# Two transformer blocks on one core: the opening steps of the weight pipeline, piece by piece and in another order

## What is computed

```
h = rms_norm(x, attn_norm_w[l])
proj = h @ w_in[l]
q, k, v, u, g = jnp.split(proj, splits, axis=-1)
...
lam = (exp(sum(lam_q1 * lam_k1)) - exp(sum(lam_q2 * lam_k2)) + lam_init)
a = diff_attention(q[0], q[1], k[0], k[1], v, lam, rel_bias)
...
u_a, u_b = jnp.split(u, 2, axis=-1)
c = causal_depthwise_conv(u_a * sigmoid(u_b), conv_w[l], conv_b[l])
```

## Time and profile before

| | us |
|---|---|
| median of 3 timed runs | 762.36 |
| lowest and highest of them | 761.44, 762.84 |
| the profiled execution | 763.56 |
| its span in the trace | 761.8 |
| PE busy in it | 736.0 (97%) |
| DVE, ACT, POOL busy | 483.4, 397.1, 174.5 |

### The profile page before, as it was taken

How to read it: one execution, slowest core, us unless ns; L and a number is a source line. 1 busy time by engine, 2 the same in 40 slices (tenths; PEclk the granted TensorE clock), 3 DMA queues, 4 the chain that set the end, 5 groups by cost and what they waited for, 6 DMA issues and landing times.

```text
span 761.8 us, 9087 instructions
## 1 busy us (share of the span) xinstructions
PE 736.0 (97%) x3430; PEld 597.5 (78%) x3430; DVE 483.4 (63%) x664; ACT 397.1 (52%) x521; POOL 174.5 (23%) x124
## 2 busy tenths in 40 slices
PE   5979999999999999999999999999999999999998
PEld 4868777777877888888888888877778888888886
DVE  4697785999967656555556354677746655653531
ACT  5544667575487455444445354569845455443330
POOL 1368899897700003000000000150001000000000
PEclk9989999999999999999999999999999999999999
DMA  9865444453536555655664656644334556455530
GB/s 292 227 189 165 154 158 160 150 192 128 186 131 247 194 166 169 197 187 170 199 198 142 218 164 195 208 141 149 111 111 160 171 166 196 167 190 192 195 138 28
DMA packets 81899, 131.44 MB, mean 173 GB/s; under 512 B 3888, under 2 KB 34632, under 8 KB 81856
## 3 DMA queue, kind: packets, MB, share of 16 engines
q1 hardware_dynamic: 81200, 129.25, 51.7%
q0 software_dynamic: 576, 1.35, 0.9%
q10 hardware_dynamic: 80, 0.26, 0.1%
HBM read 129.60 MB, written 1.25 MB: 172 GB/s over the span
## 4 chain that ended last, share of the span: by engine, by line
PE 73%; DVE 11%; ACT 9%; DMA 3%; issue 2%; POOL 1%; SPq 0%; ACTq 0%; DVEq 0%; POOLq 0%
PE acc L1535 22%; PE acc L1537 22%; PE acc L1536 22%; DVE aux L909 5%; PE aux L1216 4%; DMA raw<-w_in_dram 3%; ACT w_hi L556 3%; DVE w_lo L865 2%; PE aux L1259 1%; DVE gates L1046 1%; ACT conv L807 1%; POOL w_lo L541 0%; ACT L702 0%; ACT k_t L610 0%; DVE conv L1124 0%
## 5 line engine op out<-in xcount | busy, mean ns | idle before, releaser
L865 DVE TENSOR_TENSOR w_lo<-raw,w_hi 128x2048 fp32r<-128x2048 f32 x98 | 223.0, 2276 | 130.9 <-ACT w_hi L556 130.9
L556 ACT ACTIVATE w_hi<-raw 128x2048 fp32r<-128x2048 f32 (+1 forms) x119 | 225.7, 1899 | 144.6 <-PE acc L1537 133.4
L1535 PE MATMUL acc<-w_hi,h_hi 128*128 128x512 f32 x640 | 257.7, 403 | 7.7 <-DVE tok L920 4.4
L1537 PE MATMUL acc<-w_hi,h_lo 128*128 128x512 f32 x640 | 251.0, 392 | 0.0
L1536 PE MATMUL acc<-w_lo,h_hi 128*128 128x512 f32 x640 | 250.2, 391 | 0.0
L1535 PEld LDWEIGHTS acc<-w_hi,h_hi 128*128 128x128 f32 x640 | 121.1, 189 | 33.1 <-DVE tok L920 4.9
L1537 PEld LDWEIGHTS acc<-w_hi,h_lo 128*128 128x128 f32 x640 | 120.7, 189 | 26.4
L1536 PEld LDWEIGHTS acc<-w_lo,h_hi 128*128 128x128 f32 x640 | 121.0, 189 | 23.3
L541 POOL TENSOR_TENSOR w_lo<-raw,w_hi 128x2048 fp32r<-128x2048 f32 x21 | 96.7, 4604 | 4.7 <-ACT w_hi L556 4.7
L909 DVE SCALAR_TENSOR_TENSOR aux<-glu_t,vec_t,aux 128x256 f32<-128x256 f32 x232 | 94.3, 484 | 0.0
L446 POOL TENSOR_TENSOR rstd<-ms,nhalf 128x2 f32<-128x2 f32 x4 | 8.7, 2183 | 351.3 <-DVE ms L892 351.3
(11 more groups left out here) (218 smaller groups left out, 643.8 us busy)
## 6 DMA issues: line engine op xcount, KB each, us to landing
raw<-w_in_dram SPq DMA_DIRECT2D x30, 1024.0 KB, 5.2
raw<-w_down_dram SPq DMA_DIRECT2D x26, 1024.0 KB, 5.0
raw<-w_gate_up_dram SPq DMA_DIRECT2D x44, 512.0 KB, 4.7
raw<-w_up_dram SPq DMA_DIRECT2D x16, 1024.0 KB, 5.4
raw<-w_in_dram SPq DMA_DIRECT2D x16, 512.0 KB, 6.2
raw<-w_out_dram SPq DMA_DIRECT2D x8, 1024.0 KB, 5.1
raw<-w_proj_attn_dram SPq DMA_DIRECT2D x4, 1024.0 KB, 5.1
raw<-w_proj_conv_dram SPq DMA_DIRECT2D x4, 1024.0 KB, 5.1
```

The source lines that it names most:

```text
L556: nc.scalar.activation(w_hi[:, u % SPLIT, 0:nk, :], raw[:, u % RAW, 0:nk, :], ACT.Copy)\
L865: nc.vector.tensor_tensor(w_lo[:, u % SPLIT, 0:nk, :], raw[:, u % RAW, 0:nk, :], f(w_hi[:, u % SPLIT, 0:nk, :]), ALU.subtract).then_inc(w_ ...
L1535: nc.tensor.matmul(o, x_h, w_hi[:, slot, j, :], start=begin_, stop=False)
L1537: mm = nc.tensor.matmul(o, x_l, w_hi[:, slot, j, :], start=False, stop=end_)
```

## The change

It touches only steps 0 to 6. x is loaded by halves of its columns instead of by token tile. Units 0 and 1 are loaded by k-tile, eight DMAs of 256 KB, each with a semaphore of its own; the second half of x stands between the second and the third of them. Unit 1 is rounded and subtracted by k-tile as unit 0 is, and PE waits for it by k-tile. PE turns only pairs 0 and 1 of x ahead of unit 0, and pairs 2 and 3 in the middle of it, with the matmul of the bias table behind them (now in PSUM bank 3). ACT copies the table before unit 1, and squares x by token tile around the rounding of unit 2. DVE subtracts unit 2 ahead of the mean square. POOL writes the table to DRAM ahead of its power for `rstd`, and reads it back in steps 2 to 5 instead of 1 to 4.

```diff
@@ SP
-            for t in range(NT):
-                sp.dma_start(x_in[:, t, :], x_rows[:, t, :]).then_inc(x_loaded[t], 16)
+            def piece(u, kt):
+                c, k0 = units[u][:2]
+                _, _, w, col, pair, _, _ = chunks[c]
+                n = w.shape[-1]
+                src = bass.AP(tensor=w.tensor, offset=w.offset + (k0 + kt) * P * n + col,
+                              ap=[[n, P], [pair, 2], [1, CW // 2]])
+                sp.dma_start(raw[:, u, kt, :].rearrange("p (a b) -> p a b", a=2), src).then_inc(piece_in[UK * u + kt], 16)
+
+            for hf in range(2):
+                cols = slice(CW * hf, CW * (hf + 1))
+                sp.dma_start(x_in[:, :, cols], x_rows[:, :, cols]).then_inc(x_loaded[hf], 16)
+                piece(0, 2 * hf)
+                piece(0, 2 * hf + 1)
+            for kt in range(UK):
+                piece(1, kt)
@@ POOL
-            power(rstd[:, 0, :], ms[:, 0, :], mean_sq, 1, rstd_ready)
-            qk_epsilon(0)
-
             pool.wait_ge(rel_kept, 1)
             pool.dma_start(rel_dram.ap().rearrange("(h q r) -> h q r", h=H, q=SHIFTS), again(rel_row[:, :], SHIFTS))\
                 .then_inc(rel_stored, 16)
 
+            power(rstd[:, 0, :], ms[:, 0, :], mean_sq, 1, rstd_ready)
+            qk_epsilon(0)
+
-                for r in range(2 * s - 2, 2 * s) if 1 <= s <= step // 2 else ():
+                for r in range(2 * s - 4, 2 * s - 2) if 2 <= s <= step // 2 + 1 else ():
@@ ACT
-            def first_high(kt):
-                act.wait_ge(raw_in[0], raw_value[0])
-                nc.scalar.activation(w_hi[:, 0, kt, :], raw[:, 0, kt, :], ACT.Copy)\
+            def first_high(u, kt):
+                act.wait_ge(piece_in[UK * u + kt], 16)
+                nc.scalar.activation(w_hi[:, u, kt, :], raw[:, u, kt, :], ACT.Copy)\
                     .then_inc(first_hi if kt < UK - 1 else w_hi_ready, 1)
...
             stage_high(0, 3)
-            split_high(1)
-
-            for t in range(NT):
-                act.wait_ge(x_loaded[t], 16)
-                for hf in range(2):
...
+            act.wait_ge(rel_made, 1)
+            nc.scalar.activation(rel_row[:, :], aux[0:H, 3, 0:RELS], ACT.Copy).then_inc(rel_kept, 1)
+            for kt in range(UK):
+                first_high(1, kt)
+            row_squares(0)
+            split_high(2)
+            row_squares(1)
@@ DVE
-            split_low(1)
+            for kt in range(UK):
+                first_low(1, kt)
+            split_low(2)
             mean_square(0)
@@ PE
             def halfway(s):
+                if s == 0:
+                    stage(0, (2, 3))
+                    pe.wait_ge(consts_loaded, 32)
+                    pe.wait_ge(zeros_ready, 5)
+                    claim([3], rel_kept, 1)
+                    nc.tensor.matmul(aux[0:H, 3, 0:RELS], rel_aug[:, :], onehot[:, :], start=True, stop=True)\
+                        .then_inc(rel_made, 1)
...
-            stage(0, range(4))
+            stage(0, (0, 1))
...
-                        pe.wait_ge(*((first_lo, j + 1) if j < UK - 1 else (w_lo_dve, 1)))
+                    if s < PIECED:
+                        pe.wait_ge(*((first_lo, (UK - 1) * s + j + 1) if j < UK - 1 else (w_lo_dve, s + 1)))
```

More of the change, by code:

```diff
@@ L105, in build @@
     LEAD = 2
+    PIECED = 2
     raw_value = []
     for u, (c, *_) in enumerate(units):
[L110 removed]
+        raw_value.append((raw_value[u - RAW] if u >= RAW else 0)
+                         + (0 if u < PIECED else 16 if chunks[c][4] is None else 32))
     B = begin["x2", 0]
@@ L265, in build @@
         raw_in = [sem(f"raw_in{i}") for i in range(RAW)]
-        x_loaded = [sem(f"x_loaded{t}") for t in range(NT)]
+        x_loaded = [sem(f"x_loaded{hf}") for hf in range(2)]
+        piece_in = [sem(f"piece_in{k}") for k in range(PIECED * UK)]
         vecs_loaded, consts_loaded = sem("vecs_loaded"), sem("consts_loaded")
@@ L557, in split_high, with row_squares @@
                     .then_inc(w_hi_ready, 1)
-            def first_high(kt):
-                act.wait_ge(raw_in[0], raw_value[0])
-                nc.scalar.activation(w_hi[:, 0, kt, :], raw[:, 0, kt, :], ACT.Copy)\
+            def first_high(u, kt):
+                act.wait_ge(piece_in[UK * u + kt], 16)
+                nc.scalar.activation(w_hi[:, u, kt, :], raw[:, u, kt, :], ACT.Copy)\
                     .then_inc(first_hi if kt < UK - 1 else w_hi_ready, 1)
+            def row_squares(t):
+                for hf in range(2):
+                    act.wait_ge(x_loaded[hf], 16)
+                    if t or hf:
+                        act.wait_ge(squares, 2 * t + hf)
+                    nc.scalar.activation(junk[:, :], x_in[:, t, CW * hf:CW * (hf + 1)], ACT.Square,
+                                         accum_out=ss[:, 0, hf, t:t + 1]).then_inc(squares, 1)
             def stage_high(st, g):
@@ L583, in _ @@
                     stage_high(0, kt // 2)
[L584 removed]
+                first_high(0, kt)
             stage_high(0, 2)
             stage_high(0, 3)
[L587 to L595 removed]
+            act.wait_ge(rel_made, 1)
[5 more added lines that the diff above has]
+            row_squares(1)
             nc.scalar.activation(gains[:, 0:1], vcol(R_SUB, 0), ACT.Copy, scale=1.0 - LAM_INIT).then_inc(gains_ready, 1)
@@ L645, in _ @@
             for s in range(NU + 1):
-                if s == 1:
-                    act.wait_ge(rel_made, 1)
-                    nc.scalar.activation(rel_row[:, :], aux[0:H, 2, 0:RELS], ACT.Copy).then_inc(rel_kept, 1)
                 if s == 2:
@@ L686, in _ @@
                             .then_inc(probs_kept, 1)
-                if (s < EARLY or s >= B) and s != LN + 3 and s not in NORMS and s + LEAD < NU:
+                if (0 < s < EARLY or s >= B) and s != LN + 3 and s not in NORMS and s + LEAD < NU:
                     split_high(s + LEAD)
@@ L1080, in _ @@
                                 .then_inc(branch_sum, 1)
-                if s + LEAD < NU and s not in NORMS and s != LN + 3 and not on_pool(s + LEAD):
+                if 0 < s and s + LEAD < NU and s not in NORMS and s != LN + 3 and not on_pool(s + LEAD):
                     split_low(s + LEAD)
@@ L1232, in stage @@
                 src = x_res if st else x_in
+                if st == 0:
+                    pe.wait_ge(x_loaded[pairs[0] // 2], 16)
                 for g in pairs:
@@ L1428, in after @@
             def after(s):
-                if s == 0:
-                    pe.wait_ge(consts_loaded, 32)
-                    pe.wait_ge(zeros_ready, 5)
-                    claim([2], rel_kept, 1)
-                    nc.tensor.matmul(aux[0:H, 2, 0:RELS], rel_aug[:, :], onehot[:, :], start=True, stop=True)\
-                        .then_inc(rel_made, 1)
                 if s == 1:
@@ L1500, in _ @@
             mm.then_inc(vec_turned, 1)
-            for t in range(NT):
-                pe.wait_ge(x_loaded[t], 16)
-            stage(0, range(4))
+            stage(0, (0, 1))
             held[CONV_BANK] = (conv_done, CONV_OPS)
```

17 lines of the change are left out of this document (7 added, 10 removed).

## The result

The changed kernel takes **763.80 us** (median of 6 runs, 763.41 to 764.52) where the kernel before, in the runs beside it, takes 761.41 (6 runs, 761.06 to 762.84): a ratio of 1.0025 with a 95% interval of 1.0013 to 1.0037. Forecast were 757.6, with a range of 755.9 to 760.6. So it is 0.25% slower where it should have been 0.6% faster, and outside the range. The profiled execution has a span of 762.8, that of the kernel before had 761.8.

A forecast was written before the change was run, and what follows sets the result against it. PE, busy 97%, bounds the kernel, so gains come from its waits or clock. Unit 6 starts 3.1 us earlier, full clock saves about 3.0, POOL's limit leaves 4.8: median 762.36 becomes 757.6, range 755.9 to 760.6.

The forecast's parts named there:

- The start: Opening: with unit 0 loaded by k-tile, the first product starts near 10.8, 1.4 us earlier.
- The clock under the first products: Rival, opening: clock low until about 14 cuts the gain to 3.1 us (759.3), up to 6 us to 1.7; chance 0.13.
- The new wait for `lam`: Ahead of unit 2: PE waits about 1 us for DVE, leaving 0.2 of the 1.5 us gained.
- With the write out of the way: Middle: earlier table write helps unit 6's load take 7 us, not 13.35; DVE's idle 3.27 us goes.
- Unit 6's load by spread reads: Middle: one pair of reads beside this load instead of three; ACT rounds unit 6 at 36.1 without waiting for it.
- The gap ahead of unit 6 and its clock: Unit 6 starts at 48.9, 3.1 us earlier, behind 1.7 us of gap; clock stays full; rival that it falls: 0.07.
- The price of the low clock: Behind the gap ahead of unit 6: half clock costs products and transposes 2.5 + 0.4, about 3.0 us.
- POOL as the next bound: Ahead of unit 8: PE waits 1.25 us for `tok` of k(0), two reads adding 1.05; gain 4.8, not 6.0.
- The rival on the slower side: Middle: unit 6's load takes 13.35 us whatever the reads do, giving 763.7; late load chance 0.12, one third of it slower.

The follow-up runs named there:

- e9: e2 with the bias table's copy, write, eight reads and matmul back at their places of the kernel before; 756.04 us, 0.9931 of the kernel before.
- e2: e1 with all four pairs of x turned by PE ahead of unit 0; 759.92 us, 0.9973 of the kernel before.
- e1: Changed kernel with x loaded by token tile again, both loads ahead of unit 0's pieces; 762.14 us, 0.9997 of the kernel before.
- e7: Changed kernel with the table's copy, write, reads and matmul back at their places of before; 760.41 us, 0.9976 of the kernel before.
- e4: Kernel before with only the bias table's part of the change added; 762.88 us, 1.0012 of the kernel before.
- e3: Changed kernel with eight useless transposes on PE while it waits for the first piece; 761.73 us, 0.9998 of the kernel before.
- e11: e2 without the eight reads of the bias table, its write kept, zeros as bias; 759.46 us, 0.9964 of the kernel before.
- e5: e2 without the bias table's write and its eight reads, zeros as bias; 756.23 us, 0.9918 of the kernel before.
- e8: The kernel before, word for word, run again for a second trace; 761.66 us, ratio 0.9989.
- e10: e9 with the table's reads two by two in steps 2 to 5; 756.93 us, 0.9945 of the kernel before.

## Why the prediction was wrong, step by step

**Put together**, the runs lead from the kernel before to the changed one in four steps: the pieces and the new order on ACT and DVE (e9) -0.69%; the table part (e2 against e9) +0.42%; turning two pairs only ahead of unit 0 (e1 against e2) +0.24%; x by column halves (changed kernel against e1) +0.28%. That they add up to the measured +0.25% is so by construction and confirms nothing, and what a part is worth depends on the rest: the table part costs 0.49% in the changed kernel (e7) and 0.12% or nothing in the kernel before (e4). The first step was not split further, so no run says what of it the pieces gain and what the order. The prediction had the first part for the smaller gain, the second for the larger one, the third only as a rival, and the fourth not at all.

- **The start** (first product at 10.8). Right for the pieces, as e1 shows with 10.68. The step that failed is one that isn't there: the prediction looked at bytes ahead of the first piece of unit 0, not at what PE waits for first, `vecs`, which is loaded beside x. PE begins on it at 7.49 instead of 5.94, which put the whole opening back by 1.5.
- **The clock under the first products.** Rival, with a chance of 0.13 and priced at 3.1 us for up to 6 us of half clock. It happened, with 5.25 us, and costs 2.1 us by e3. The size was right, and the chance was low for what was to be seen: "Against it: all 24 products from 12.20 to 17.83 ran at 0.23" leaned on one trace, in which PE had turned 16 tiles before, not 8. In the three traces with 8 tiles and an idle PE behind them (changed kernel, e1, e7) the clock rose 3.8 to 5.5 us after the first product. In the ten with 16 it rose before the first product in three and up to 2.8 us after it in the others, so the 8 tiles lengthen a slow stretch that can come without them.
- **The new wait for `lam`.** It exists and decides nothing: 0.47 in the changed kernel, 0.42 in e1 and 0.18 in e2, where about 1 us was forecast.
- **"With the write out of the way"**: the step that failed worst. The prediction let the write vanish from where it was and costed it at nothing where it came to. It had stood behind SP's request for unit 4 and now stands ahead of it, and the prediction did not ask which load it would run beside. It was unit 4's: ACT's rounding of unit 4, forecast at 25.45, came at 30.79 behind a wait of 1.81, and at 26.60 behind one of 2.06 where the start was in time (e2). The write by itself is worth 0.46% (e11 against e5). In the kernel before the write hit unit 5's load instead (8.3 us, asked for 1.7 after the write), whose delay shows in the earlier trace rows as DVE's 2.31.
- **Unit 6's load by spread reads.** The changed kernel shows what was forecast (rounding at PE's release, 40.29, no hole on DVE), so a comparison of two traces would have confirmed the cause. e7 and e9, with the reads where they were before, deny it for these openings: unit 6's load is in time without the spreading. What made the 13.35 us of the earlier trace rows stays open. In e4, on the kernel before, the table part took them to 8.9, but it also moved the request 2.5 us back, so it is not shown to be the reads. Of the traces it can be said that in the kernel before unit 6 was asked for 1.3 us ahead of the reads and behind a unit 5 that was late, and in e9 3.9 us ahead of them behind one that took 6.5 us.
- **The gap ahead of unit 6 and its clock.** "1.7 us of the gap stay", and the clock with them: right in all five traces with such a gap (see the last section). The changed kernel didn't get there (2.95). The price of the low clock, about 3.0 us, was read rightly from the trace and is too high for the median run. The trace has 6.8 us of it, and most runs of the kernel, by their mean clock, 3.4 (e8). With 3.4 us, as in e2, the 12 products and 8 transposes at unit 6 take 5.2 us, at full clock 3.7 (e9), so that the price is 1.6. The gain should not have been taken off the median whole: e9 is 7.2 us earlier than the kernel before in the traces and 5.3 us faster in the times.
- **POOL as the next bound.** Right. In e10 PE waits 1.32 for `tok` ahead of unit 8 (forecast 1.25), and e9 shows that this is the price of the two reads (forecast 1.05). In the changed kernel `tok` of k(0) is done at 67.29 and unit 8 starts at 67.58, 12 products ahead of 70.30: 0.3 us of slack are left of 2.7.

The rival on the slower side was a late load of unit 6 whatever the table did. What came was a late load of unit 4, because of the table.

## What to carry to other kernels

A transfer that is moved out of one load's way is moved into another's: list the requests within some microseconds on either side of its new place and ask who waits for each. In an opening, follow first what the first instruction of the critical engine waits for, and what shares the DMA engines with it. A change of four parts that comes out near zero may hold a gain and three losses; undoing one part at a time finds it, where a comparison of two traces would have named the wrong cause.
